# Expert weights in four places, asked for four blocks ahead, and 24 filled-in blocks instead of 20, in an encoder block on one Trainium2 core

## The reference, cut to what matters

```
s1, s2 = scores of x @ wq against 128 + 128 subkeys
ids    = 16 best pairs of each of 8 heads and 256 tokens, of 128*128 experts
g      = softmax(vals, axis=-1)
a      = jnp.einsum('td,thkd->thk', xt, u_tab[ids])
hid    = (jax.nn.gelu(a.astype(jnp.float32)) * g).astype(xt.dtype)
y_peer = jnp.einsum('thk,thkd->td', hid, v_tab[ids])
x      = layer_norm(DN_ALPHA * x + y_peer, ln2_g[l], ln2_b[l])
```

## Time and profile before

| what | value |
|---|---|
| median of three executions | 1076.23 us (1074.82 to 1078.57) |
| the profiled execution's own time | 1079.52 us |
| its span in the trace | 1077.5 us |
| mean granted TensorE clock | 0.988 |
| TensorE busy | 1040.4 us (97%) |
| VectorE busy | 841.6 us (78%) |
| ScalarE busy | 453.6 us (42%) |
| GpSimd busy | 450.2 us (42%) |

### The profile page before, as it was taken

How to read it: one execution, slowest core, us unless ns; L and a number is a source line. 1 busy time by engine, 2 the same in 40 slices (tenths; PEclk the granted TensorE clock), 3 DMA queues, 4 the chain that set the end, 5 groups by cost and what they waited for, 6 DMA issues and landing times.

```text
span 1077.5 us, 20423 instructions
## 1 busy us (share of the span) xinstructions
PE 1040.4 (97%) x6781; PEld 931.3 (86%) x6781; DVE 841.6 (78%) x1529; ACT 453.6 (42%) x652; POOL 450.2 (42%) x332
## 2 busy tenths in 40 slices
PE   8999999899999999999999999978999999999995
PEld 8878898899999999999999999626777777788884
DVE  4465557687999999988888888227888988888887
ACT  4384434344434434444444444104444444444441
POOL 3910000048888888788888888780000000000000
PEclk9999999999999999999999999998999999999998
DMA  9776688544766666977777777788788887888782
GB/s 318 247 259 217 215 285 295 200 118 99 139 142 144 143 137 137 199 177 171 172 166 169 168 172 174 188 244 264 253 252 251 257 259 247 253 252 241 239 244 95
DMA packets 152514, 220.93 MB, mean 205 GB/s; under 512 B 48032, under 2 KB 98528, under 8 KB 152480
## 3 DMA queue, kind: packets, MB, share of 16 engines
q1 hardware_dynamic: 115040, 219.07, 64.4%
q0 software_dynamic: 37440, 1.43, 9.7%
HBM read 202.48 MB, written 17.96 MB: 205 GB/s over the span
## 4 chain that ended last, share of the span: by engine, by line
POOL 38%; PE 32%; issue 10%; DMA 10%; DVE 9%; ACT 1%; DVEq 0%; SPq 0%; POOLq 0%; ACTq 0%
POOL expert_weights L509 38%; PE ps L1380 15%; PE ps L1283 14%; DMA g_in<-expert_weights 9%; DVE g_in L1060 2%; DVE hid_lo L1067 1%; DVE hid_hi L1065 1%; DVE v_lo L1051 1%; DVE w_lo L962 1%; PE ps L1173 1%; DMA expert_weights<-gw,cell 1%; PE ps L1151 1%; ACT w_hi L632 1%; DVE xres L755 0%; DMA xres<-in_x_dram 0%
## 5 line engine op out<-in xcount | busy, mean ns | idle before, releaser
L509 POOL DMA_INDIRECT expert_weights<-gw,cell x256 | 412.4, 1611 | 256.1 <-DVE gw L949 170.6
L1324 PE MATMUL ps<-act_hi,uT_hi 128*128 128x256 f32 x1024 | 295.1, 288 | 0.0
L1324 PE MATMUL ps<-act_hi,uT_lo 128*128 128x256 f32 x1024 | 289.9, 283 | 0.0
L1324 PE MATMUL ps<-act_lo,uT_hi 128*128 128x256 f32 x1024 | 289.7, 283 | 0.0
L710 ACT ACTIVATE v_hi<-v_raw 128x512 fp32r<-128x512 f32 x256 | 147.8, 625 | 224.5 <-PE ps L1380 178.7
L1324 PEld LDWEIGHTS ps<-act_lo,uT_hi 128*128 128x128 f32 x1024 | 196.6, 192 | 0.0
L1324 PEld LDWEIGHTS ps<-act_hi,uT_hi 128*128 128x128 f32 x1024 | 196.6, 192 | 0.0
L1324 PEld LDWEIGHTS ps<-act_hi,uT_lo 128*128 128x128 f32 x1024 | 196.3, 192 | 0.0
L1051 DVE TENSOR_TENSOR v_lo<-v_raw,v_hi 128x512 fp32r<-128x512 f32 x256 | 164.8, 685 | 5.7 <-ACT v_hi L710 5.7
L1380 PE MATMUL ps<-v_hi,hid_hi 128*128 128x512 f32 x472 | 149.3, 398 | 15.3 <-DVE hid_lo L1067 14.8
L1380 PE MATMUL ps<-v_hi,hid_lo 128*128 128x512 f32 x472 | 146.5, 392 | 0.0
(11 more groups left out here) (156 smaller groups left out, 1431.1 us busy)
## 6 DMA issues: line engine op xcount, KB each, us to landing
v_raw<-in_peer_v_dram SPq DMA_DIRECT2D x148, 512.0 KB, 4.3
u_raw<-in_peer_u_dram SPq DMA_DIRECT2D x68, 512.0 KB
u_raw<-in_peer_u_dram SPq DMA_DIRECT2D x240, 128.0 KB, 2.8
w_raw<-in_w_in_dram SPq DMA_DIRECT2D x8, 2048.0 KB, 8.9
expert_weights<-zeros SPq DMA_DIRECT2D x16, 1024.0 KB, 12.1
g_in<-expert_weights SPq DMA_DIRECT2D x108, 128.0 KB, 3.2
w_raw<-in_peer_wq_dram SPq DMA_DIRECT2D x4, 2048.0 KB, 10.8
w_raw<-in_w_out_dram SPq DMA_DIRECT2D x2, 2048.0 KB, 9.6
```

Source lines behind the costliest of these rows:

```text
L509: pool.indirect_dma_start(out=table_cells, out_offset=bass.IndirectOffsetOnAxis(ap=cell[:, t, k:k + 1], axis=0), in_=gw[:, t, k:k + 1], in ...
L1324: ins = pe.matmul(ps[:, bank, 0:T], (uT_hi, uT_hi, uT_lo)[part][:, slot, k, :], (act_hi, act_lo, act_hi)[part][:, k, :], start=(k == 0 and ...
```

## The change

`g_in` gets four places instead of two, at 1 KB to 5 KB of the kernel's area, where `act_hi` (the inputs of expert_inputs, not read after those) was. Block m's weights go to place m % 4, each place with a semaphore of its own, and the load for block m + 4 is asked for after hidden(m). The first three weight loads and the first half load are issued together after `scattered1`. `FILLS` goes from 20 to 24. The list of SyncE loses its special round at the border and its last two loads.

```diff
-FILLS = 20
+FILLS = 24
...
-    g_in = sb("g_in", [P, 2, T], 201 * K1)
+    g_in = sb("g_in", [P, BODY, T], 1 * K1)
...
                 sp.wait_ge(s["scattered1"], 16 * SLOTS)
-                for b in range(2):
+                for b in range(BODY - 1):
                     load_g(b, b)
+                load_g_second(FILL_BLOCK, BODY - 1)
...
                 sp.wait_ge(s["hid_done"], BODY * i + (k + 1))
-                (load_g_second if k == 1 and g_blocks is not whole else load_g)(g_blocks(i, k + 2), k % 2)
+                (load_g_second if k == 3 and g_blocks is mixed else load_g)(g_blocks(i, k + BODY), k)
...
-        next_inputs(FILLS - 1, border, border)
-        with sp.Fori(FILLS, NB // BODY - 2) as i:
+        with sp.Fori(FILLS - 1, NB // BODY - 2) as i:
             next_inputs(i, whole, whole)
         next_inputs(NB // BODY - 2, whole, whole, BODY - AHEAD)
-        for k in range(2):
-            sp.wait_ge(s["hid_done"], NB - BODY + k + 1)
-            load_g(FILL_BLOCK - BODY + k + 2, k)
-
...
-        def hidden(m, b, slot, landed, head, second):
+        def hidden(m, b, place, landed, head, second):
 
             c = P if second else 0
-            cells = g_in[:, slot, c:T]
-            dve.wait_ge(s[f"g_in{slot}"], landed)
+            slot = place % 2
+            cells = g_in[:, place, c:T]
+            dve.wait_ge(s[f"g_in{place}"], landed)
...
-                hidden(BODY * i + k, b, k % 2, 32 * i + 16 * (k // 2 + 1), head and k < 2, mixed and k == 3)
+                hidden(BODY * i + k, b, k, 16 * i + 16, head and k < 2, mixed and k == 3)
```

More of the change, by code:

```diff
@@ L249, in hybrid_block @@
              "act_hi_done", "act_lo_done", "pq_first", "pqT_first", "key_scores", "sc_copied", "soft_in", "soft_exp", "route_done",
-             "zero_set", "zeroed", "scattered0", "scattered1", "g_in0", "g_in1",
+             "zero_set", "zeroed", "scattered0", "scattered1", "g_in0", "g_in1", "g_in2", "g_in3",
              "g_fill_in0", "g_fill_in1", "g_fill_in2", "g_fill_in3", "fill_hid", "fill_done",
@@ L418, in whole @@
             return BODY * i + (k - FILLS)
-        def border(i, k):
-            return mixed(i, k) if k < BODY else whole(i, k)
         with sp.Fori(0, FILLS - 2) as i:
```

## The result

| what | before | after |
|---|---|---|
| median | 1076.92 us (4 runs, 1074.82 to 1078.57) | 1064.08 us (4 runs, 1063.15 to 1064.71) |
| ratio, after to before | | 0.9884, 95% interval 0.9865 to 0.9903 |
| profiled execution's own time | 1079.52 us | 1063.89 us |
| its span | 1077.5 us | 1061.9 us |

The change makes the kernel 12.8 us faster, between 10.4 and 14.5 us by the interval. The forecast was 1061.8 us.

The account below looks back on a forecast made before the run. Weight waits were taken to bound the mixed rounds, TensorE the whole ones. Gains of 10.6 and 5.45 us, less 1.9 of slip and 0.2 of rounding, give 1065.1 us; less the 3.3 us offset, 1061.8, range 1058 to 1069.

Parts of the forecast that it names:

- The mixed rounds: Main rounds of 42 matmuls: look-ahead of four ends VectorE's weight waits, 9.55 us a round instead of 10.11.
- the 745 named: Sign in the profile: TensorE's unbroken chain of matmuls begins near 745 us in place of 935.79.
- the first (half lost to a new wait): Mixed rounds: something else replaces the wait, half the gain lost, 9.83 us a round, 1068.3 us; chance 0.10.
- the second (not what bound): Mixed rounds: look-ahead was not the bound, rounds stay 10.11 us, only half blocks gained, 1074.7 us; chance 0.05.
- The half blocks: Main rounds: four more fills turn four whole rounds into mixed ones, 5.45 us less.
- The slip of the start: Start of the main rounds: added fills delay scatter, weights and V, 1.9 us later, bounds nothing to 3.5 us.
- V of block 1 landing just ahead: Start: V of block 1 arrives just before the first main block, forecast at 732.8 and up to 732.9 us.
- The low clock: TensorE's half clock in block 0: costs or gives almost nothing, since block 1 can't start before 738.5 us anyway.
- The offset: Whole execution: the profiled run's 3.3 us above the median, subtracted from 1065.1 us to give the forecast median.
- The third rival: Rounds and start: transfers bound the rounds, added bytes take 8.3 us, rounds stay 10.11 us, 1081.1 us; chance 0.03.

Follow-up runs that it names:

- e3: The changed kernel, four places and 24 fills kept, with each weight load asked for two blocks ahead instead of four: 1075.5 us, ratio 0.9991.
- e4: The changed kernel, four places and 24 fills kept, with each weight load asked for three blocks ahead instead of four: 1062.0 us, ratio 0.9854.
- e8: The changed kernel with 16 filled-in blocks instead of 24, loads still asked for four ahead: 1071.9 us, ratio 0.9967.
- e2: The changed kernel with 20 filled-in blocks instead of 24, so the look-ahead of four alone: 1065.3 us, ratio 0.9898.
- again: The changed kernel itself, nothing altered, measured and profiled a second time: 1063.7 us, ratio 0.9889 against the kernel before.

## Why the prediction was right

The forecast was 1061.8 us in 1058 to 1069, and 1064.1 was measured; 14.4 us less were forecast, 12.8 measured, and 14.4 lies within the interval's 10.4 to 14.5.

1. *The mixed rounds.* Forecast 9.55 us instead of 10.11, by TensorE's own price; measured 9.52 in every profile with three or four ahead, and the unbroken chain began at 737.98, earlier even than the 745 named. Two, three and four blocks ahead with the same four places (e3, e4, after) show that the time between asking and need was the cause. Of the rivals, the first (half lost to a new wait) falls with the waits table, and the second (not what bound) falls with e3 beside e4: the loads took 3.7 us at the median in the rounds, after the change as before. The estimate of 2.3 us for 128 KB by the Trainium skill, "DMA: Bandwidth & Descriptors", section "Anatomy of one DMA — SWDGE (gpsimd) path", which stood beside that rival, is near the 1.9 to 2.0 us of a quiet queue and doesn't hold under this traffic; it is from a fit for DMAs that GpSimd issues, and SyncE issues these.
2. *The half blocks.* 5.45 us forecast. e8 to e2 gave 4.7 us where the pause was long, near the full price.
3. *The slip of the start.* 1.9 us forecast, within 0 to 3.5. From the first fill matmul to the end of hidden(4), the mean over three profiles with 20 fills and two ahead is 59.3 us. With 24 fills and four ahead it is 60.8 and 62.7. So 1.5 and 3.4 us, a mean of 2.5: the term was somewhat short. Two things in its working failed. The scatter was bounded by 1.9 us of delay, and took 3.5 us more than in the quiet (6.51 against 3.03). That the first main block still came at 732.88, where 732.8 was forecast, is luck: the last scatter was issued 1.84 us earlier in this execution (723.11 against 724.95), which hid the excess. And the aside, "V of block 1 landing just ahead", was the second chain, and it was last in "again". The low clock, costed at almost nothing, cost nothing only in the profile where block 1 waited for V (737.98). In "again" hidden(1) was done at 737.1 and block 1 had to wait for TensorE itself, at half speed, until 739.98.
4. *The offset.* The forecast carried the profiled execution's 3.3 us above the median over as it was. The difference does lie mostly ahead of the rounds, by the two further profiles, but it did not carry over: the changed kernel's profile was 0.2 us below its median. From profile to profile 14.4 us were forecast and 15.6 measured, from median to median 12.8. So this term, with 0.7 us by which the median before rose with its fourth run (1076.23 to 1076.92), is why the forecast is 2.3 us too low while the profile of the changed kernel came out 1.2 us faster than its forecast (1063.9 against 1065.1). The mechanism has no part in that. From the first fill matmul on, the three profiles of before end at 382.0 us in the mean and the two of after at 368.3: 13.7 us less.
5. *The third rival* (transfers bound the rounds) falls: 270 GB/s were moved in the rounds with no wait for them.

## What to carry to other kernels

A prefetch needs to be as deep as its landing time under the traffic of that stage is long, measured from the point where the load can be asked for to the point of need; asking one block earlier than that gave nothing here, and a half-size block between the two shortens the distance just there. (Three places, asked for three ahead, was not run.) A filler in a pause is worth its full price only as long as the pause is long; near its end every fill delays what the next stage needs (its buffers, its share of the queue), so the optimum is flat. And the price of the bounding engine, taken from a stretch where it never waits, told within 0.03 us what a round would take once its waits were gone. Last, when a load is late, look first at what stands ahead of it in the issuing list: the time between the last scatter's issue and the weights' own was the scatter's landing in some of these kernels and the wait for V's place in others.

## What the runs showed of the hardware that was not expected

- A scatter of 128 cells issued by GpSimd took 3.03 us to land in the quiet and 6.51 us at 314 GB/s of other traffic. Over all profiles it was 3.0 to 3.4 us without and 4.8 to 6.5 us with the added fills' loads. With 28 fills, the weights were asked for 9.7 us after its issue, but it had landed after 5.6 us; the rest is the wait for the fills' places, which stands ahead of them in the list.
- A 128 KB load with nothing ahead of it in the queue landed in 1.9 us, in the same place behind two loads of 512 KB in 5.2 us.
- All nine profiles with three or four blocks ahead have rounds that repeat at 9.51 to 9.53 us from the third on. In the five with two ahead, the single rounds spread from 9.4 to 10.8 us. The spread went with the waits.
